# Attention steps inside a unit of weights, between its products with the high and the low part

## The reference, cut to what matters

```python
proj = jnp.einsum('bsd,dc->bsc', h, w_in[layer])          # 256 x 2048 times 2048 x 8200
q, k, v = qkv[0], qkv[1], qkv[2]                          # 4 mixers x 8 heads x 64
gate = proj[..., 3 * MIX_WIDTH:4 * MIX_WIDTH]
o_a = dilated_attention(rope(norm(q[0])), rope(norm(k[0])), v[0])
o_b = stick_breaking_attention(q[1], k[1], v[1])
o_c = moba_attention(rope(norm(q[2])), rope(norm(k[2])), v[2])
o_d = forgetting_attention(norm(q[3]), norm(k[3]), v[3], log_f)
y = concat(o_a, o_b, o_c, o_d) * jax.nn.silu(gate)
x = x + jnp.einsum('bsc,cd->bsd', y, w_out[layer])
```

## Time and profile before

| | us |
|---|---|
| median of 3 runs (lowest, highest) | 3103.57 (3100.7, 3106.92) |
| profiled execution, its own time | 3102.1 |
| span of its trace | 3100.3 |
| PE busy over the span | 3035.3 (98%) |
| DVE busy, ACT busy | 1700.8 (55%), 1479.7 (48%) |
| the two `rest` stretches in the trace | about 2152 to 2479, and 2678 to 3007 |

### The profile page before, as it was taken

The page is one execution under the profiler, slowest core; times in us unless marked ns, Lnnn a source line. Parts: engine busy times, 40 slices in busy tenths (PEclk is TensorE's granted clock), DMA queues, the critical chain, the costliest instruction groups (busy, mean ns, idle before and its releaser), DMA issues.

```text
span 3100.3 us, 38533 instructions
## 1 busy us (share of the span) xinstructions
PE 3035.3 (98%) x14336; PEld 2512.8 (81%) x14336; DVE 1700.8 (55%) x1802; ACT 1479.7 (48%) x1835; POOL 218.1 (7%) x205
## 2 busy tenths in 40 slices
PE   8989999999999989899999999999999999999999
PEld 7878888888888778688888888888887888888787
DVE  5654454455445775454455444557546555755654
ACT  5554444444445454454444444454555545555553
POOL 1000000000000220000000000003300000510000
PEclk9999999999999999899999999999999999999999
DMA  8536666665556525366666666566544455644445
GB/s 268 186 115 192 188 187 192 187 188 189 191 192 196 162 84 177 114 184 191 189 187 187 191 188 192 188 195 191 156 144 141 150 183 178 189 146 147 143 156 170
DMA packets 278432, 542.12 MB, mean 175 GB/s; under 512 B 16640, under 2 KB 18720, under 8 KB 277664
## 3 DMA queue, kind: packets, MB, share of 16 engines
q1 hardware_dynamic: 276352, 531.30, 56.2%
q0 software_dynamic: 1952, 9.06, 0.8%
HBM read 537.15 MB, written 3.15 MB: 174 GB/s over the span
## 4 chain that ended last, share of the span: by engine, by line
PE 61%; ACT 2%; DVE 1%; issue 0%; ACTq 0%
PE ps L412 15%; PE ps L459 11%; PE ps L880 10%; PE ps L420 8%; PE ps L436 5%; PE ps L887 5%; PE ps L1068 1%; PE ps L1007 1%; PE ps L1046 1%; PE ps L985 1%; ACT w_hi L354 0%; PE ps L720 0%; PE ps L661 0%; PE ps L854 0%; ACT qkT L991 0%
## 5 line engine op out<-in xcount | busy, mean ns | idle before, releaser
L361 DVE TENSOR_TENSOR w_lo<-w_raw,w_hi 128x1024 fp32r<-128x1024 f32 x1008 | 1269.2, 1261 | 1306.2 <-ACT w_hi L354 1301.6
L354 ACT ACTIVATE w_hi<-w_raw 128x1024 fp32r<-128x1024 f32 x1008 | 1066.8, 1059 | 1494.7 <-PE ps L420 656.8
L880 PE MATMUL ps<-w_hi,actT_hi 128*128 128x512 f32 x1408 | 550.0, 391 | 0.0
L880 PE MATMUL ps<-w_hi,actT_lo 128*128 128x512 f32 x1408 | 547.9, 389 | 0.0
L887 PE MATMUL ps<-w_lo,actT_hi 128*128 128x512 f32 x1408 | 376.5, 389 | 0.0
L412 PE MATMUL ps<-w_hi,hidT_hi 128*128 128x512 f32 x928 | 363.1, 391 | 2.3 <-DVE hidT_lo L689 2.3
L412 PE MATMUL ps<-w_hi,hidT_lo 128*128 128x512 f32 x928 | 361.2, 389 | 0.0
L459 PE MATMUL ps<-w_hi,actT_hi 128*128 128x512 f32 x768 | 310.1, 404 | 4.1 <-ACT pall L481 3.5
L887 PEld LDWEIGHTS ps<-w_lo,actT_hi 128*128 128x128 f32 x1408 | 264.3, 188 | 55.1
L880 PEld LDWEIGHTS ps<-w_hi,actT_lo 128*128 128x128 f32 x1408 | 264.4, 188 | 54.2
L880 PEld LDWEIGHTS ps<-w_hi,actT_hi 128*128 128x128 f32 x1408 | 264.4, 188 | 54.1
(11 more groups left out here) (264 smaller groups left out, 2696.8 us busy)
## 6 DMA issues: line engine op xcount, KB each, us to landing
w_raw<-ffn_w_in SPq DMA_DIRECT2D x352, 512.0 KB, 3.6
w_raw<-w_in SPq DMA_DIRECT2D x256, 512.0 KB, 3.5
w_raw<-ffn_w_out SPq DMA_DIRECT2D x176, 512.0 KB, 3.7
w_raw<-w_out SPq DMA_DIRECT2D x64, 512.0 KB, 3.7
w_raw<-attn_w_in SPq DMA_DIRECT2D x48, 512.0 KB, 3.6
w_raw<-xattn_w_kv SPq DMA_DIRECT2D x32, 512.0 KB, 6.0
w_raw<-attn_w_out SPq DMA_DIRECT2D x32, 512.0 KB, 3.7
w_raw<-xattn_w_q SPq DMA_DIRECT2D x16, 512.0 KB, 3.7
```

The costliest lines, as they stand in the source:

```text
L354: nc.scalar.activation(w_hi[:, v % NS], w_raw[:, v % NS], ACT.Copy).then_inc(w_hi_done, 1)
L361: nc.vector.tensor_tensor(w_lo[:, v % NS], w_raw[:, v % NS], w_hi[:, v % NS].bitcast(F32), ALU.subtract).then_inc(w_lo_done, 1)
L880: nc.tensor.matmul(ps[:, 2 * b + tb], lhs[:, k, tb * P:(tb + 1) * P], w_hi[:, s, kk * CB:(kk + 1) * CB], start=(k == 0 and part == 0), sto ...
```

## The change

In `pe_rest`, which is used by both `rest` stretches and by nothing else, the call `mid(8 * e + j)` moves. For j = 0 to 6 PE now issues the eight products with the high part, then the attention steps of the position with their waits, then the wait for `w_lo_done` and the four products with the low part, whose last one increments `w_used`. For j = 7 the order stays. ACT's and DVE's programs are unchanged.

```diff
                     if whole:
+
+                        mid(8 * e + j)
                         pe.wait_ge(w_lo_done, us + 1)
                         for tb in range(TB):
                             mm = pe_rest_low(tb, j, s)
                     mm.then_inc(w_used, 1)
-                    mid(8 * e + j)
+                    if not whole:
+                        mid(8 * e + j)
```

## The result

The changed kernel is slower: 3126.19 us, the median of 4 runs (3124.54 to 3128.05), against 3103.52, the median of 4 runs of the kernel before (3100.7 to 3106.92). The ratio is 1.0076 with a 95% interval of 1.0064 to 1.0089. The forecast was 3121 with a range of 3113 to 3129; it held, 5 short. The profiled execution took 3125.58 with a span of 3123.8, so in the traces the change costs 23.5. (From L480 on its lines are numbered 3 higher than before: L1256 is now L1259, L991 is L994, and so on.)

What follows compares the result with a forecast made beforehand. PE's instructions plus its few waits were taken to bound the kernel. New waits of 8.97 us a layer, 17.9 over both layers, made 3120.0 from the profiled 3102.1; 1.5 more to the median gave 3121, range 3113 to 3129.

Steps and rivals of the forecast that it cites:

- The rule for neighbours: Neighbouring positions: PE waits input-ready time after T (a unit's last low product issued), plus 0.06, minus 1.81 us.
- 42, 44, 45, 48, 66 and 75: PE waits added per layer: 0.50 us each at 42, 44, 45; 0.53 at 48; 1.16 at 66; 0.91 at 75.
- 43: Position 43: PE waits for DVE's division of unit 7, 1.37 us a layer.
- 84: Position 84: PE's values step waits for a full copy on ACT, 0.50 us a layer.
- 17, 25, 33: Positions 17, 25, 33: the probabilities wait for ACT's full copy behind the job's copy, 0.50 us each a layer.
- 52 to 62: Positions 52 to 62, the z and r steps: PE 1.25 us behind at the end per layer, bounds 0 and 1.82.
- The switch, taken as 0: Moved steps in both stretches: a step costs PE the same ahead of low products as ahead of high ones, 0 us.
- the bound of 5.1: Scores and z on 64 rows, 30 in all: each saves 0.17 us or pays it once more, 5.1 either way.
- the rival of 15.0: All 88 moved step positions each save 0.17 us, 15.0 in all; chance of faster by more than 0.2%: 0.03.
- my two cases: Clock falls in the rest stretches: none added in the forecast; five more in the rival, 8 us, giving 3129.
- no change: Rest stretches: new waits absorbed, or half come and switching saves 5.1; within 0.2%, 6.2 us; chance 0.07.
- The clock rival: Rest stretches: new PE waits make the granted clock fall, 1.63 us a fall, total 3127 to 3139 us; chance 0.14.

Runs made afterwards that it cites:

- The second experiment: Kernel before with only 21 step positions per layer, the close pairs with both partners, moved ahead of their low products: 3121.15 us, ratio 1.0062.
- the first experiment: Kernel before with only 28 of the 44 step positions per layer moved ahead of their low products: 3102.35 us, ratio 1.0000.
- the last fence of the experiments above: ACT's timeline in the kernel before with ACT's root of the norms at 58 and DVE's L1301 of piece 2 at 58: 3094.44 us, ratio 0.9978.

## Why the prediction held, and where it was off

- **What bounds the kernel.** Right: PE's instructions plus its waits. The only other term that showed is PE's own clock.
- **The rule for neighbours** (ready after T, plus 0.06, minus 1.81). Right to 0.05 at 42, 44, 45, 48, 66 and 75, and to 0.09 at 43; the rows at 43 to 45 above show each piece of it. Only 84 came out at 0.65 for 0.50; 0.1 of that shows at PE's next step, at 88, and the cause stays open.
- **17, 25, 33.** The mechanism was right and the size was off: 0.50 each, measured 0.72 to 0.75. I took the split of 16 as starting 0.26 after T and did not ask what the moved scores of 14 do to ACT's exponentials at 15. The second experiment, without that move, gives the 0.50.
- **52 to 62.** 1.25 forecast, 1.2 to 1.4 measured once the falls are taken off, although I built it up from several half-known slacks. The steps on the way hold too: the forecast had PE 1.58 behind at r of 60 and 1.25 at r of 62, and the traces have 1.62 and 1.58 at 60, 1.39 and 1.22 at 62. The bounds of 0 and 1.82 were wider than was needed.
- **The switch, taken as 0.** Right, and shown by the first experiment, for steps on 64 rows too (the z by the steps behind them, -0.03 and -0.02). The price of 0.17 that the bound of 5.1 and the rival of 15.0 were made from was misread: a z isn't a job on fewer rows. It has as many products, but four of them have 256 columns (L1246 and L1248 above), where the job's eight have 128. So 1.10 against 0.93 doesn't show what a switch costs, and no row did.
- **The clock.** This is what was left out of the sum. I had it as a rival with 0.14 and priced one fall at 1.63, which the later traces confirm (1.65); the count was between my two cases, three falls net instead of none or five. A better sum would have carried an expected number of falls as a term: the two waits of 2.3 before had brought one, and the new order has six waits a layer above 1, three of them of 1.7 or more in the end. The range held because its upper side left room for five falls, 8: the 2.0 by which the waits were too small and the 4.95 of the three falls both came out of that, and 1.3 was given back by chance outside the stretches. My sign for it, the clock's row below 0.97, was too coarse: three falls in a stretch of 340 lower it only to 0.98.
- **Outside the stretches** nothing changed but for 1.3 between two executions.
- **The rivals.** Switching, in either direction, fell with the first experiment; "no change" fell with the result. The clock rival is a part of the truth, some 5 of 23.5. Its step that the four short waits in a row at 42 to 45 would bring falls is wrong: see below.

By these terms: 19.9 of waits (17.9 forecast), 4.95 of falls (none in the sum), and -1.3 elsewhere.

## What to carry to other kernels

When a step is moved on an engine that is never idle, its own time doesn't matter; what matters is which semaphore increment it is now ahead of, and what the other engines have queued behind the wait for that increment. Write down for each neighbouring pair the time from the release to the consumer's need, and check it three positions back as well; pairs with slack (28 of 44 here) can be moved for nothing, pairs without lose what the sum says, here to within 0.15 where all that feeds them had been looked at (17, 25 and 33, where it had not, lost half as much again). If the order on the busy engine must be so, let the followers do the awaited step ahead of work that has three units of slack.

## What the runs showed of the hardware

**The clock and the length of a wait.** In the traces of all ten kernels PE has 34 waits of 1.7 or more in the two stretches. At or right behind 15 of them the granted clock is 0.50 for a while, and PE loses about 1.65; at the other 19 it stays at full clock. The same place goes either way from one layer to the next. The timeline of r at 60 and at 62 in the first layer of the changed kernel shows one of each:

```profile
2367.87 0.84 PE L1259 MATMUL ps<-stW,low 128*128 128x256 f32 x2 [2.35 <-DVE stW L1304]
2368.51 0.64 PE L1260 MATMUL ps<-stW,tri 128*128 128x128 f32 x2
...
2379.09 0.70 PE L1259 MATMUL ps<-stW,low 128*128 128x256 f32 x2 [2.09 <-DVE stW L1304]
2379.62 0.38 PE L1260 MATMUL ps<-stW,tri 128*128 128x128 f32 x2
```

Behind none of the waits of 1.24 or less in the two stretches did the clock fall (there are none between 1.24 and 1.7), also not at 42 to 45, where four waits (0.35, 1.24, 0.30, 0.30) follow each other within 15 us. The Trainium skill, "TensorE: Matmul & The Clock Gate", section "A second HAM failure mode: psum-queue depth-cycling", has frequent micro-idles bring such swings; the four at 42 to 45 did not. The size of a single wait may not be all, though: in the first block, which the change doesn't touch, PE of the changed kernel waits 2.75, 1.11, 1.41, 1.32 and 3.28 between 1274.8 and 1292.3, the clock is 1.00 from 1285 to 1289, which takes in the wait of 1.32, and 0.50 from 1289.7 on, when the wait of 3.28 has run for 0.7. No run tells whether the last wait or the row of shorter ones ahead of it brings that. What decides whether a long wait brings a fall stays open.

**A step costs the same between high and low products as between units**, on 64 rows too: 56 moves in the first experiment, 0.05 each at most, and the z at 45 and 56 in the changed kernel.

**A switch of ACT's table is short here.** In the last fence of the experiments above Exp ends at 2313.98, the load begins at 2314.00 and takes 1.28, and Ln starts at 2315.30. The Trainium skill, "ScalarE: Activation LUTs", section "What ACT_TABLE_LOAD costs", counts a drain of about 1.38 on top, 2.66 in all; this trace shows no such time between the two, and 46 of its 50 loads have less than 0.1 on either side; the measurement decides.
